# Ten weight slots filled in one order through the whole program, and row dots beside every search but the first

## The reference

```python
q = (xb @ w_query).reshape(-1, PEER_HEADS, 2, PEER_QHALF)
s = jnp.einsum('thpd,pkd->thpk', q, sub_keys)
sv, si = lax.top_k(s, 16)                       # best 16 of 128 keys, on each of two sides
cand = sv[:, :, 0, :, None] + sv[:, :, 1, None, :]
top_s, top_p = lax.top_k(cand, 16)              # best 16 of the 256 sums: 16 of 16384 experts
g = jax.nn.softmax(top_s, axis=-1)
u = u_tab[eidx]
act = jax.nn.gelu(jnp.einsum('thkd,td->thk', u, xb))
return jnp.einsum('thk,thkd->td', g * act, v_tab[eidx])
```

## Time and profile before

| | us |
|---|---|
| median of three runs | 1716.95 |
| the profiled execution itself | 1719.39 |
| its span | 1717.6 |
| TensorE busy (96% of the span) | 1641.6 |
| VectorE busy (63%) | 1090.1 |
| GpSimd busy (28%) | 485.5 |
| ScalarE busy (12%) | 212.8 |
| moved by DMA | 533.85 MB, mean 311 GB/s |

### The profile page before, as it was taken

The page is one execution under the profiler, slowest core; times in us unless marked ns, Lnnn a source line. Parts: engine busy times, 40 slices in busy tenths (PEclk is TensorE's granted clock), DMA queues, the critical chain, the costliest instruction groups (busy, mean ns, idle before and its releaser), DMA issues. The chain is left out here.

```text
span 1717.6 us, 33684 instructions
## 1 busy us (share of the span) xinstructions
PE 1641.6 (96%) x12244; PEld 1526.3 (89%) x12244; DVE 1090.1 (63%) x2433; ACT 212.8 (12%) x617; POOL 485.5 (28%) x423
## 2 busy tenths in 40 slices
PE   9999999899999999999899999999999999999997
PEld 7687899898999999888788888988899999989997
DVE  3362379984699997455546415999359999844442
ACT  2251221111110000000004312111111100000000
POOL 0000001363244446333410001133334444533320
PEclk9999999999999999999899999999999999999999
DMA  4213478999999999999973436799999999999984
GB/s 146 98 62 127 137 267 284 353 373 360 348 408 399 385 398 409 409 410 410 409 273 133 144 127 220 256 355 352 384 353 361 400 391 397 396 402 393 409 340 156
DMA packets 149911, 533.85 MB, mean 311 GB/s; under 512 B 17617, under 2 KB 20434, under 8 KB 149842
## 3 DMA queue, kind: packets, MB, share of 16 engines
q1 hardware_dynamic: 89938, 314.90, 49.0%
q0 software_dynamic: 59904, 218.13, 32.8%
HBM read 531.92 MB, written 1.05 MB: 310 GB/s over the span
## 5 line engine op out<-in xcount | busy, mean ns | idle before, releaser
L236 PE MATMUL ps<-big,raw 128*128 128x160 f32 (+2 forms) x5232 | 844.7, 321 | 25.0 <-DMA raw<-in_u 23.7
L236 PEld LDWEIGHTS ps<-big,raw 128*128 128x128 f32 x5232 | 776.4, 190 | 78.7 <-issue 21.2
L1095 PE MATMUL ps<-big,raw 128*128 (+1 forms) x4096 | 599.6, 303 | 22.4 <-DMA raw<-in_v_rows 7.9
L1095 PEld LDWEIGHTS ps<-big,raw 128*128 128x128 f32 x4096 | 562.9, 190 | 49.8 <-issue 46.7
L1138 POOL DMA_INDIRECT big<-in_u_rows,big x208 | 254.8, 1225 | 858.3 <-DVE big L1264 410.3
L1281 DVE SCALAR_TENSOR_TENSOR big<-big 128x1024 f32<-128x1024 f32 x201 | 258.0, 1283 | 201.7 <-PE ps L1095 105.6
L1138 POOL DMA_INDIRECT big<-in_v_rows,big x208 | 227.5, 1094 | 311.6 <-DVE big L1281 251.1
L1264 DVE CUSTOM_DVE_ANT_0 big<-big 128x1024 f32<-128x1024 f32 x208 | 243.8, 1218 | 9.9 <-DMA big<-in_u_rows,big 9.9
L1178 ACT ACTIVATE big<-ps 128x160 f32 x256 | 77.9, 304 | 547.9 <-PE ps L236 522.4
L1212 DVE MAX8 big<-big 128x8 f32<-128x128 f32 (+1 forms) x99 | 33.6, 339 | 103.5 <-ACT big L1147 91.1
L321 ACT ACTIVATE big<-h 128x272 f32<-128x272 f32 (+1 forms) x32 | 12.6, 419 | 622.9 <-DVE h L1355 572.6
(11 more groups left out here) (165 smaller groups left out, 723.3 us busy)
## 6 DMA issues: line engine op xcount, KB each, us to landing
raw<-in_u SPq DMA_DIRECT2D x256, 512.0 KB
raw<-in_v_rows SPq DMA_DIRECT2D x256, 512.0 KB
raw<-in_query SPq DMA_DIRECT2D x32, 512.0 KB, 3.3
raw<-in_lru_w SPq DMA_DIRECT2D x24, 512.0 KB, 3.4
raw<-in_mla_down SPq DMA_DIRECT2D x17, 512.0 KB, 3.3
raw<-in_mla_out SPq DMA_DIRECT2D x8, 512.0 KB, 3.6
big<-in_u_rows,big POOLq DMA_INDIRECT x208
big<-in_v_rows,big POOLq DMA_INDIRECT x208
```

The costliest lines, as they stand in the source:

```text
L236: mm = pe.matmul(out, self.mem.raw[:, s, c * P:(c + 1) * P], x[:, c, :], start=(c == 0), stop=(c == DC - 1))
L1095: return pe.matmul(accumulator(c), mem.raw[:, s, c * P:(c + 1) * P], act_w[:, i, :], start=start, stop=False, skip_group_check=True)
```

## The change

`raw` gets ten slots. All weight tiles of the program, from the first of `mla_down` to the last `v` tile of layer 1, stand in one list, and tile g of that list goes to slot g % 10. A new class `Tiles` has the semaphores for all stages; SyncE runs at most ten tiles ahead of TensorE, also across stages. The room comes from `big`, whose size is now taken from the stage that needs most. The loops over tiles on SyncE, TensorE and ScalarE are written out. Six dots now follow every search but the first, and a dot waits for its copy of the tokens (`reps_out`) where it is the first of its 16. In the first half of the gates rows stop at the last dot (`ROWS`). In layer 0 the folds 0, 1 and 2 now stand before tiles 112, 116 and 120 of `v`, in layer 1 folds 0 and 1 before 112 and 116; the last stays before 124.

```diff
-UNROLL = 4
+SLOTS = 10
-ROWS_PER_FIND, ROWS_AT_SPREAD, ROWS_PER_GROUP, LAST_ROW_TILE = 6, 9, (2, 2), 118
-BIG = NK * L
+ROWS_PER_FIND, ROWS_AT_SPREAD, ROWS_PER_GROUP, LAST_ROW_TILE = 6, 9, 2, 118
+BIG = NK * max(L - GATHERED[0], SEQ - GATHERED[1]) + 8 * D
...
-        self.raw = sb("raw", [P, UNROLL, D])
+        self.raw = sb("raw", [P, SLOTS, D])
...
+class Tiles:
+    def __init__(self, ctx, mem, tiles):
+        self.mem, self.tiles = mem, tiles
+        self.landed = [ctx.sem(f"landed{k}") for k in range(SLOTS)]
+        self.done = ctx.sem("tiles_done")
+
+    def fetch(self, sp, first, last):
+        for g in range(first, min(last, len(self.tiles))):
+            if g >= SLOTS:
+                sp.wait_ge(self.done, 2 * (g - SLOTS + 1))
+            sp.dma_start(self.mem.raw[:, g % SLOTS, :], self.tiles[g]).then_inc(self.landed[g % SLOTS], 16)
...
-    def multiply_raw(self, pe, turn, s, out, x, scaled=None):
-        pe.wait_ge(self.landed[s], turn * 16 + 16)
-        pe.wait_ge(self.free[s % 2], turn * 2 + (s // 2 + 1))
+    def wait_landed(self, pe, n):
+        g = self.base + n
+        pe.wait_ge(self.mem.tiles.landed[g % SLOTS], 16 * (g // SLOTS + 1))
+
+    def multiply_raw(self, pe, n, out, x, scaled=None):
+        self.wait_landed(pe, n)
+        pe.wait_ge(self.free[n % 2], n // 2 + 1)
...
-            with sp.Fori(U0 + 1, V0) as turn:
-                for s in range(UNROLL):
-                    st.load_read(sp, turn, s, tile_of(d["u"][layer], turn - U0, s))
-            with sp.Fori(V0, END) as turn:
-                for s in range(UNROLL):
-                    st.load_read(sp, turn, s, tile_of(v_tiles, turn - V0, s))
+            mem.tiles.fetch(sp, st.base + SLOTS, st.base + PEER_TILES + SLOTS)
...
             def dot(n):
                 wait_row(n)
+                if n % TOPK == 0:
+                    dve.wait_ge(reps_out, 2 * copy_of(n) + 2)
...
                 find(first, min(2, G - first))
-                if first >= GG:
+                if first:
                     n = rows(n, n + ROWS_PER_FIND)
...
                 for m in range(NG):
-                    n = rows(n, n + ROWS_PER_GROUP[half])
+                    n = rows(n, n + ROWS_PER_GROUP if half else min(n + ROWS_PER_GROUP, ROWS))
...
-            u_tiles(U0, SPREAD)
+            for i in range(SPREAD):
+                u_product(i)
...
-            with pe.Fori(SCATTER, V0) as turn:
-                for s in range(UNROLL):
-                    u_product(turn, s)
-                    if s in GROUPS_AFTER:
-                        products(pe, 0, (turn - SCATTER) * 2 + GROUPS_AFTER.index(s))
+            for i in range(SCATTER, NK):
+                u_product(i)
+                if i % 2:
+                    products(pe, 0, (i - SCATTER) // 2)
...
-            folds = {END - 4: range(0, COPIES - 1), END - 1: [COPIES - 1]}
+            fold_before = {NK - 16 + 4 * b: b for b in range(COPIES - 1)}
+            fold_before[NK - 4] = COPIES - 1
```

## The result

The changed kernel takes 1636.38 us, the median of four runs (1634.76 to 1637.01). The kernel before takes 1719.09 us beside it, and the ratio is 0.9517 (95% interval 0.9485 to 0.9549). Predicted was 1640, in a range of 1616 to 1670. The profiled execution spans 1634.5 us, 83.1 less than before.

The account below looks back on a forecast made before the run. The prediction took the DMA engines, shared equally by tiles and rows, to bound layer 0's end. Gains of 45 and 36 us less 3 for the clock made 78 off 1719.4; it said 1640 us, range 1616 to 1670.

Parts of the forecast that it names:

- The loss per layer, 66 and 39 us, and its upper bound of 105: First u tile to last fold: time beyond TensorE's own 588 us, 66 in layer 0, 39 in layer 1; at most 105 recoverable.
- 45 + 36 - 3 = 78: Whole kernel: layer 0 gains 45 us, layer 1 gains 36, a lower TensorE clock costs 3; 78 us saved.
- VectorE is late at the spread of layer 0: Layer 0's spread: 18 added dots make TensorE wait 4.3 us for VectorE; rival with VectorE as bound: 1660 us, chance 0.10.
- Beside the 40 groups, 203.5: First to last gate product: 39 steps of 5.18 us plus 1.5 for the turn from u to v, 203.5 us.
- The end of layer 0, 197 us: Last gate product to last fold of layer 0: 162 pieces on the DMA, less those in hand, 197 us (188.6 to 204.5).
- six more tiles in hand: Start of layer 0's end: up to six more weight tiles already fetched, taking 7.7 us off it.
- A moved row is worth 1.28 us: Layer 0's end: each row moved out saves one DMA piece, 1.28 us; 18 rows save 23.
- No cost from fetching instructions: Written-out code: 73 more instruction blocks cost nothing; rival that they starve TensorE: 1787 us, chance 0.04.
- Without the loops, 39 groups at 5.18: Gate products in written-out code: each step runs at TensorE's own 5.18 us instead of 5.29.
- The clock, 3 us: Layer 0: two waits of 4 to 5 us may lower TensorE's clock, costing 3 us (0 to 10).
- The rest, 0: Ahead of 228 us and between the layers, and in SyncE's loads and the dots' new wait: no change, 0 us.

Follow-up runs that it names:

- later_exp: Changed kernel with the search's table hot moved behind place, so ScalarE's wait for VectorE stands after u tile 78 instead of 72; 1637.9 us, 0.9511 of the kernel before.
- slots_only: Changed kernel with its ten slots, but six dots only after the searches that had them before; 1670.3 us, 0.9771 of the kernel before.
- dots_only: Changed kernel with four slots instead of ten, moved dots kept; 1705.3 us, 0.9980 of the kernel before.
- written_out_only: Changed kernel with four slots and dots only after the searches that had them before; 1717.0 us, 1.0041 of the kernel before.
- slots_only_rows_first: slots_only with SyncE fetching the next stage's weights only when all rows of layer 0 have been used; 1666.1 us, 0.9685 of the kernel before.
- before_again: The kernel before, unaltered, traced a second time; that run took 1753.7 us at a mean clock of 0.944.
- seven_slots: Changed kernel with seven slots instead of ten; 1649.1 us, 0.9584 of the kernel before.

## Why the prediction was right, step by step

**The loss per layer, 66 and 39 us, and its upper bound of 105:** right in size; 79 of them came back. Layer 1 lost all of its loss, 40.0 against the 36 I took and a bound of 39. I had kept 3 us for small waits that did not occur. The layers gave 79.0 us where 45 + 36 - 3 = 78 was forecast, in part by luck: 6 us too few in layer 0 met 4 too many in layer 1. The 4.3 us ahead of the first layer, which the forecast put at nothing, make it 83.

**VectorE is late at the spread of layer 0:** right. Counted from the first `u` tile, the spread was forecast at 187.4 and came at 188.5; the first gate product at 207.1 and came at 207.6, behind a wait of 4.55 us (5.2 forecast). One wait on the way was missed, and so the wait at the spread itself was 0.56 us instead of 4.3. ScalarE waits for VectorE (`shifted`) behind tile 72 before it takes the next tile, and I read that point only as VectorE waiting for ScalarE, as in the earlier trace rows. With 18 dots more it turned round: VectorE reached it at 385.6, tile 72 was done at 381, ScalarE stood, both product banks stayed full and TensorE waited 2.88 us. later_exp shows that it cost 1.4 us at most by itself, as TensorE waits at the spread anyway. ScalarE's exponential in the changed kernel:

```profile
385.69 0.43 ACT L1137 ACTIVATE big<-big 128x272 f32<-128x272 f32 x1 [3.30 <-DVE big L1255]
```

**Beside the 40 groups, 203.5:** measured 204.7 (636.43 - 431.71), and 202.1 in layer 1.

**The end of layer 0, 197 us:** measured 838.9 - 637.3 = 201.6. This is the term that was too low: 4.6 of the 6 us by which layer 0 gained 39 instead of 45; 1.2 more are the groups. I took six more tiles in hand as there at its start. TensorE went at its own pace for about 80 us of the end, which is 37 tiles while 31 or 32 came; so by an estimate five or six were in hand and not ten, and four missing at 1.28 us are 5.1. Between the nine dots and the 40 groups, where four pieces need 5.12 of 5.18 us, there was no time to fill them all.

**A moved row is worth 1.28 us:** right for the change as it was made and wrong as a rule. From slots_only to the changed kernel layer 0 gets 23.3 us shorter for 18 rows, 1.29 each; but that is 36.6 us less in the end and 13.2 more ahead of it, where I had the 23 in the end alone, so the agreement is in part luck. I weighed the equal shares of the earlier trace rows, but the sum goes by pieces, as if either queue could use what the other leaves. It can't always: with four slots a row less at the end is worth 0.80 us (dots_only against written_out_only), with ten slots and no moved dots the rows are late instead (slots_only). The Trainium skill's rule of turns between queues ("DMA: Bandwidth & Descriptors", Queues, rings and completion order) agrees with two of these: slots_only, where VectorE does wait for its rows, has 51.2% for either queue, and in slots_only_rows_first six tiles less on the one queue brought the last fold 6.3 us forward.

**No cost from fetching instructions:** right as far as a trace shows; 73 more blocks forecast, 66 seen, and no wait on them. The Trainium skill, "Runtime: NRT & Kernel Launch" (Instruction fetch mechanics), has block crossings mostly hidden; here they were, beside DMA engines at a share of 1.03. Open is why written_out_only was 7.1 us slower than before beside it. **Without the loops, 39 groups at 5.18:** right; written_out_only has it with four slots, 202.5 and 202.1 us. **The clock, 3 us:** two stretches of 3.4 us at half speed, after the waits of 2.88 and 4.55 us, so 3.4 us. **The rest, 0:** most likely right; the 4.3 us look like one execution's.

## What to carry to other kernels

Where two queues fill the DMA engines, price a transfer by who is short: with equal shares, taking bytes off one queue helps the other only as far as it has buffers to run ahead, and deeper buffers help only if the other queue's work is not then the last. So look for the pair (depth, and work moved into a quiet stretch) before you judge either edit alone: in the layer spans 3.8 and 48.2 us apart, 79.0 together. And when an engine gets more work ahead of a handshake, ask at each point where it used to wait whether the other side now waits, and what is queued behind that.

## What the runs showed of the hardware

Between the start and the last fold TensorE's granted clock fell to half only at waits of 1.9 us and more (before_again, lower throughout, is left aside), and it stayed there for 3.4 us (behind the wait of 2.88 us in the changed kernel) to 27.3 us (around the wait of 26.24 in slots_only). But not each such wait had it: in seven_slots the granted clock was 1.00 behind waits of 2.84 and 3.44 us, and in dots_only behind all its waits for tiles, up to 2.0 us. Two queues that were both behind got 51.2% each, 409 GB/s together (slots_only, 660 to 840 us). One execution of the changed kernel took 4314.8 us, with a granted clock given as 1.00 throughout: TensorE took 50.76 us for its first five tiles (80 records), which take 18.50 in the other trace of the same kernel. Nothing in its trace says why, and it occurred once.
